# By rows out of a layer: two projections of a transformer kernel give tokens in rows, and the norms behind them are postponed

## The chip, the cores and the metric

One NeuronCore of a Trainium2 chip runs the whole program. The metric is the device time of one execution in microseconds; the median of several runs is given. The engines are TensorE (PE: matmul, with PEld for its weight loads), VectorE (DVE), ScalarE (ACT), GpSimd (POOL) and SyncE (SP), which issues the DMAs.

## What is computed

A transformer of three layers on 256 tokens of width 1024, all in fp32. The first layer (block 1) has three kinds of attention and a gated feed-forward with a causal convolution; the next two (block 2) are modulated by a condition vector `c`. Only the ends of the first layer and the start of the second matter here:

```python
def rmsnorm(x, g):
    y = xf * lax.rsqrt(jnp.mean(xf * xf, axis=-1, keepdims=True) + EPS) * g

# first_block
mixed = concatenate([rmsnorm(out_a, g_a), rmsnorm(out_b, g_b), rmsnorm(out_c, g_c)])
x = x + rmsnorm(mixed @ w_out, attn_post_norm)
h = rmsnorm(x, ffn_pre_norm)
u = causal_depthwise_conv(h @ w_up, conv_w, conv_b)      # 3 taps, 5632 columns
gate, up = split(u, 2)
x = x + rmsnorm((gelu(gate) * up) @ w_down, ffn_post_norm)  # 2816 -> 1024

# second_block, for layer in 0, 1
shift_m, scale_m, gate_m, shift_f, scale_f, gate_f = split(silu(c) @ ada_w + ada_b, 6)
h = rms_norm(x, norm_gains[layer, 0]) * (1 + scale_m) + shift_m
x = x + gate_m * mixer(h)          # layer 0: w_qkv, attention, w_o
h = rms_norm(x, norm_gains[layer, 1]) * (1 + scale_f) + shift_f
x = x + gate_f * swiglu(h)         # gate_up, down
```

## The kernel before

**Layout.** Activations stand turned: a tile is 128 features on the partitions by S = 256 tokens, and x is DT = 8 such tiles. A matrix product takes a 128 x 128 block of weights as the stationary operand and streams 256 tokens. For accuracy each fp32 operand is split in two reduced-precision parts, `hi` (a rounded copy, made by ACT) and `lo` (the remainder, made by DVE), and each product is three matmuls: hi x hi, lo x hi, hi x lo (L1334 to L1336). PE's time is the count of these matmuls.

**Chunks.** Weights come in chunks. `PHASES` lists the layers in order with their chunks: w_in 10, w_out 5, up 22, down 16, qkv 12, att_o 4, gu0 22, dn0 16, ret_in 24 and so on. For each chunk SP issues a load into a ring of raw buffers (L582), ACT makes `w_hi` from it (L729), DVE `w_lo` (L2014), each in two halves of up to 1024 columns, and PE then works the chunk: for a chunk of 1 MB 48 matmuls of 256 columns. `hi(chunk)` and `lo(chunk)` are the two splits; each engine's order is written out by hand, and they stand one chunk ahead. A load waits till the raw buffer's last chunk is split.

**PSUM.** The eight banks are `lin[0:2]`, `sco[0:2]`, `tra[0:2]` and `att[0:2]`. A layer's chunks use `lin` in turn. A chunk's bank is free once its reader has left it: in up that are DVE's convolution taps (L2249).

**Up.** For each pair of feature tiles ACT starts the convolution (L964 on) from the bank, DVE adds two taps for each tile, ACT makes gelu, GpSimd (two chunks of three) or DVE multiplies by the up half (L652), and ACT rounds the hidden tile (L993), GpSimd takes its remainder (L662). The modulation of block 2 is worked in 48 pieces of 1 MB, spread over the layers (`ADA_STEPS`): SP loads a piece (L572) after the chunk's weights, waiting till DVE has finished the piece two before, and DVE makes two products with sums (L2098) and a small addition behind the chunk's split and taps.

**Norms.** A norm needs the sum of squares of each token, over the partitions. ACT squares each tile, PE multiplies it by ones into one column (`sums`, L1431), DVE refines 1/sqrt from ACT's root and writes two 128 x 128 diagonals of the factors (L2023 to L2030), and PE multiplies ones by these (`spread`, L1443), which gives the factors on all partitions. In between PE runs fillers on constant data (`keep_busy`, L1412). The residual norms POST (behind w_out) and FFNPOST (behind down) then scale y by the factors and add it to x, tile by tile (L2078). Behind each follows another norm of the new x: FFNPRE before up, L0 before qkv, again with squares, sums, factors, spread, and for each of eight tiles scale, round, remainder. Up's and qkv's chunk 0 goes by feature tiles in the order in which these are ready.

**Postponed norms.** Three norms further on (`DEFERRED`: L0F before gu0, L1, L1F) are treated another way. The next layer's chunks 0 to 2 run on z = x * gain, not normalised, with banks of their own (L1709 `start_chunk`). Chunk 0 has the sums at one of its 16 places, chunk 1 has the spread at its place 0 (L1731 `deferred_phase`). ACT copies the factors (`rbc_copy`) and the three chunks' banks into SBUF (`leave_first`, L1112), and GpSimd multiplies these six tiles by the factors (`settle`, L682). Meanwhile DVE scales eight tiles of h (L2324, L2329), with chunk 2's split after tiles 4 and 6 and chunk 3's behind them (L2313), and from chunk 3 on the layer runs on h. GpSimd adds the squares of the tiles first (L642), so that fewer sums stand on PE.

**Order around w_out.** The last group of mixed tiles (late norm GROUP_F) comes during w_out's first two chunks; its spread stands behind two chunks of 36 matmuls. The loads of up wait for its last tile, since up's buffers lie where these were made.

## Time and profile before

| | us |
|---|---|
| median of 3 runs | 1107.26 |
| lowest and highest of them | 1104.3, 1260.35 |
| the profiled execution as a run | 1108.74 |
| its span (first to last instruction) | 1106.9 |
| mean granted TensorE clock in it | 0.989 |

The profile is one execution. Its page gives busy time of each engine, a picture of the span in 40 slices, DMA queues, the chain of work that ended last, groups of instructions and DMA issues. Durations below come from it. The trace also answers for single instructions (a timeline) and for stretches (windows). A busy PE may be doing fillers, and a matmul's shown duration overlaps the next one's: the pace is the distance between starts. In the windows "PEclk" is the granted clock, 1.00 for 2.4 GHz and 0.50 for 1.2 GHz, and the DMA share is the mean over the core's 16 DMA engines.

### The profile page before, as it was taken

The numbers are of one execution on the slowest core, as the hardware profiler recorded it, in microseconds if no ns is written. First come the engines' busy times: TensorE is split into PE (matmuls) and PEld (weight loads), VectorE is DVE, ScalarE is ACT, GpSimd is POOL, SyncE is SP. The second block draws the span as 40 slices with busy tenths as digits, with TensorE's granted clock in tenths as the row PEclk, the third lists the DMA queues.
The fourth block names the chain that finished last, engine by engine and source line by source line (L and its number), as shares of the span: only waits on it lengthen the run. The fifth ranks groups of instructions, "written<-read, shape, count | busy, mean of one in ns | idle before, by whom it ended". The sixth has DMA issues, their size and how long they took to land.

```text
span 1106.9 us, 21659 instructions
## 1 busy us (share of the span) xinstructions
PE 1065.8 (96%) x8385; PEld 1027.9 (93%) x8385; DVE 792.3 (72%) x1375; ACT 596.0 (54%) x1016; POOL 142.3 (13%) x146
## 2 busy tenths in 40 slices
PE   6989999999989999999999999999999999999998
PEld 5878899999989999799999999997899999999997
DVE  5767658999978788768887788877467657554443
ACT  6576446776444456657544444633465556544442
POOL 0000012434310000003211101300010013111010
PEclk9999989999999899999999999999999999999999
DMA  9621263767498553345797778454334454554450
GB/s 365 222 86 68 77 259 154 295 239 287 166 363 321 227 215 128 115 176 179 304 353 281 282 291 332 173 215 162 143 138 148 179 183 153 190 189 154 159 182 38
DMA packets 34399, 226.66 MB, mean 205 GB/s; under 512 B 3827, under 2 KB 4124, under 8 KB 12444
## 3 DMA queue, kind: packets, MB, share of 16 engines
q1 hardware_dynamic: 33884, 223.11, 53.8%
q0 software_dynamic: 448, 2.63, 0.6%
q8 instruction: 45, 0.74, 0.3%
q14 instruction: 22, 0.18, 0.0%
HBM read 224.66 MB, written 2.63 MB: 205 GB/s over the span
## 4 chain that ended last, share of the span: by engine, by line
PE 77%; DVE 9%; ACT 5%; DMA 5%; issue 2%; POOL 1%; SPq 0%; DVEq 0%; ACTq 0%; POOLq 0%
PE psum L1334 21%; PE psum L1336 20%; PE psum L1335 20%; DVE w_lo L2014 3%; DMA raw<-in_down 2%; PE psum L1399 2%; PE psum L1402 2%; PE psum L1401 2%; PE psum L1412 2%; DVE arena L2098 2%; ACT w_hi L729 2%; PE psum L1431 1%; POOL arena L682 1%; DMA raw<-in_qkv 1%; DMA raw<-in_up 1%
## 5 line engine op out<-in xcount | busy, mean ns | idle before, releaser
L2014 DVE TENSOR_TENSOR w_lo<-raw,w_hi 128x1024 fp32r<-128x1024 f32 (+1 forms) x354 | 395.9, 1141 | 202.4 <-ACT w_hi L729 195.5
L729 ACT ACTIVATE w_hi<-raw 128x1024 fp32r<-128x1024 f32 (+1 forms) x354 | 338.3, 971 | 264.6 <-PE psum L1336 201.7
L1334 PE MATMUL psum<-h_hi,w_hi 128*128 128x256 f32 (+1 forms) x1240 | 355.3, 287 | 6.8 <-DVE w_lo L2014 3.0
L1335 PE MATMUL psum<-h_lo,w_hi 128*128 128x256 f32 (+1 forms) x1240 | 349.2, 282 | 0.0
L1336 PE MATMUL psum<-h_hi,w_lo 128*128 128x256 f32 (+1 forms) x1240 | 347.9, 281 | 0.0
L1334 PE MATMUL psum<-hid_hi,w_hi 128*128 128x256 f32 (+1 forms) x1096 | 311.8, 284 | 14.2 <-DVE w_lo L2014 7.7
L1336 PE MATMUL psum<-hid_hi,w_lo 128*128 128x256 f32 (+1 forms) x1096 | 309.9, 283 | 0.0
L1335 PE MATMUL psum<-hid_lo,w_hi 128*128 128x256 f32 (+1 forms) x1096 | 309.6, 283 | 0.0
L1334 PEld LDWEIGHTS psum<-h_hi,w_hi 128*128 128x128 f32 x1240 | 233.4, 188 | 11.2 <-issue 5.8
L1335 PEld LDWEIGHTS psum<-h_lo,w_hi 128*128 128x128 f32 x1240 | 234.5, 189 | 0.7 <-issue 0.7
L1336 PEld LDWEIGHTS psum<-h_hi,w_lo 128*128 128x128 f32 x1240 | 234.5, 189 | 0.0
L1334 PEld LDWEIGHTS psum<-hid_hi,w_hi 128*128 128x128 f32 x1096 | 207.3, 189 | 16.9 <-issue 11.1
L1336 PEld LDWEIGHTS psum<-hid_hi,w_lo 128*128 128x128 f32 x1096 | 207.1, 189 | 0.0
L1335 PEld LDWEIGHTS psum<-hid_lo,w_hi 128*128 128x128 f32 x1096 | 207.0, 189 | 0.0
L2098 DVE CUSTOM_DVE_ANT_0 arena<-arena 128x1024 f32<-128x1024 f32 x96 | 124.3, 1331 | 0.0
L642 POOL TENSOR_TENSOR arena<-arena 128x256 f32<-128x256 f32 x29 | 29.4, 1013 | 475.4 <-ACT arena L1102 322.2
L993 ACT ACTIVATE hid_hi<-arena 128x256 f32 (+1 forms) x60 | 25.1, 418 | 79.2 <-DVE arena L2259 63.4
L662 POOL TENSOR_TENSOR hid_lo<-arena,hid_hi 128x256 f32 (+1 forms) x44 | 35.9, 816 | 181.6 <-ACT hid_hi L993 173.4
L1412 PE MATMUL psum<-busy 128*128 128x256 f32 x221 | 40.3, 343 | 2.5 <-ACT busy L768 2.5
L652 POOL TENSOR_TENSOR arena<-arena 128x256 f32<-128x256 f32 x22 | 31.2, 1419 | 86.5 <-ACT arena L982 86.5
L1412 PEld LDWEIGHTS psum<-busy 128*128 128x128 f32 x221 | 36.4, 246 | 3.0 <-ACT busy L768 2.5
L2249 DVE SCALAR_TENSOR_TENSOR arena<-psum,cols,arena 128x255 f32<-128x255 f32 (+1 forms) x88 | 36.3, 473 | 1.7 <-ACT arena L972 1.1
(245 smaller groups left out, 1024.9 us busy)
## 6 DMA issues: line engine op xcount, KB each, us to landing
arena<-in_ada SPq DMA_DIRECT2D x48, 1024.0 KB, 4.9
raw<-in_gu SPq DMA_DIRECT2D x44, 1024.0 KB, 4.8
raw<-in_ret_in SPq DMA_DIRECT2D x24, 1024.0 KB, 4.8
raw<-in_up SPq DMA_DIRECT2D x22, 1024.0 KB, 7.0
raw<-in_dn SPq DMA_DIRECT2D x32, 704.0 KB, 5.5
raw<-in_qkv SPq DMA_DIRECT2D x12, 1024.0 KB, 7.8
raw<-in_down SPq DMA_DIRECT2D x16, 704.0 KB, 7.1
raw<-in_ret_o SPq DMA_DIRECT2D x8, 1024.0 KB, 4.7
```

The source lines that it names most:

```text
L642: nc.gpsimd.tensor_tensor(acc, acc, sq[:, k * S:(k + 1) * S], ALU.add).then_inc(sq_added, 1)
L652: nc.gpsimd.tensor_tensor(hid, ff["u"][:, 2 * at + S:2 * at + 2 * S], ff["g"][:, at:at + S], ALU.mult)\
L662: nc.gpsimd.tensor_tensor(hid_lo[:, cut], ff["hid"][:, S * (j % 2):S * (j % 2) + S], hid_hi[:, cut].bitcast(F32), ALU.subtract).then_inc(h ...
L729: nc.scalar.activation(w_hi[chunk % SPLIT_SLOTS][:, a:b], raw[chunk % RAW_SLOTS][:, a:b], ACT.Copy)\
L993: nc.scalar.activation(hid_hi[:, bass.ds(step.n(lambda c: (c - lag) * S), S)], ff["hid"][:, S * (j % 2):S * (j % 2) + S], ACT.Copy).then_i ...
L1334: nc.tensor.matmul(out, w[0], hc, start=start, stop=False, skip_group_check=True)
L1335: nc.tensor.matmul(out, w[0], lc, start=False, stop=False, skip_group_check=True)
L1336: return nc.tensor.matmul(out, w[1], hc, start=False, stop=stop, skip_group_check=True)
L1412: nc.tensor.matmul(bank[:, 0:S], busy[:, 0:P], busy[:, :], start=True, stop=True)
L2014: tt(w_lo[s][:, a:b], raw[chunk % RAW_SLOTS][:, a:b], w_hi[s][:, a:b].bitcast(F32), ALU.subtract)\
L2098: ins = nc.vector.tensor_tensor_reduce(w, w, cond_silu, 1.0, 0.0, ALU.mult, ALU.add, sums[:, b:b + 1])
L2249: ins = stt(u[:, back:S], bank[:, S * s:S * s + S - back], w, u[:, back:S], ALU.mult, ALU.add)
```

## The change

1. **Rows.** w_out (4 chunks now) and down (11 chunks of 1 MB, before 16 of 704 KB) use the activation tiles as the stationary operand (128 features x 128 tokens) and stream 512 columns of weights: `by_rows`. The result has tokens on the partitions and stands in four banks: rows 0 in `sco`, rows 1 in `lin`. In the last chunk the banks are finished one after the other.
2. **The residual norms** POST and FFNPOST are gone as norms. ACT squares each bank with an accumulation along the row (`row_squares`), DVE makes the factors (`row_residual`) and a diagonal for each 128 tokens; copies of the rows (`row_copies`) are multiplied by the diagonals on PE, 16 fp32 matmuls of 128 columns (`turn_rows`), which turns them back into feature tiles and normalises them. x gets turned * gain, tile by tile.
3. **The norms behind them**, FFNPRE and L0, join `DEFERRED`. As DVE updates each tile of x, ACT makes z's hi part and the square, and DVE the lo part. For these two the sums stand at place 1 and the spread at place 11 of chunk 1. In up the first three chunks' convolution reads the settled tiles (`conv_settled`, `taps_settled`), in qkv `settle_heads` makes q and k of them, and the first attention scores move from chunks 3 and 4 to chunk 4.
4. **Pieces.** Up has a piece at chunks 5, 6, 7, 9, 11 ... 19, 20, 21 (before: each odd one), down one at each of chunks 0 to 9 (before 11 over 16 chunks), qkv none (before 3), gu0 one at each of chunks 4 to 20 (before 13).

```diff
-    ("w_in", 10, DT, 2, 1), ("w_out", 5, DT, 2, 1),
-    ("up", 22, DT, 2, 1), ("down", 16, HALF, 1, 2),
+    ("w_in", 10, DT, 2, 1), ("w_out", 4, DT, 2, 1),
+    ("up", 22, DT, 2, 1), ("down", 11, DT, 2, 1),
...
-ADA_STEPS = [("w_in", 10, lambda c: int(c in (KA, QA0))), ("up", 22, lambda c: c % 2), ("down", 16, lambda c: int(c % 2 or c in (0, 2, 12))),
-             ("qkv", 12, lambda c: int(c < 3)),
-             ("gu0", 22, lambda c: int(4 <= c <= 20 and (c % 2 or c in (4, 6, 8, 18, 20)))), ("dn0", 16, lambda c: c % 2)]
+ADA_STEPS = [("w_in", 10, lambda c: int(c in (KA, QA0))), ("up", 22, lambda c: int(c >= 5 and c % 2 or c in (6, 20))),
+             ("down", 11, lambda c: int(c < 10)), ("gu0", 22, lambda c: int(4 <= c <= 20)), ("dn0", 16, lambda c: c % 2)]
...
-NORM_GROUPS = [[8], [2, 1], [4, 2], [2], [8], [8], [8], [8], [8], [8], [8], [8]]
+NORM_GROUPS = [[8], [2, 1], [4, 2], [2], [], [8], [], [8], [8], [8], [8], [8]]
...
-DEFERRED = (L0F, L1, L1F)
+DEFERRED = (FFNPRE, L0, L0F, L1, L1F)
...
+            def row_squares(ph, i):
+
+                stage = ROW_STAGE[i]
+                for r in range(2):
+                    for n in range(2):
...
+                        at = 28 + 2 * n + r
+                        nc.scalar.activation(e0["sq"][:, (2 * r + n) * 512:(2 * r + n + 1) * 512], row_bank(ph, r, n)[:, :], ACT.Square,
+                                             scale=D ** -0.5, accum_out=row_stat[:, at:at + 1]).then_inc(row_sq, 1)
+                act.wait_ge(row_ms, stage + 1)
+                nc.scalar.activation(row_stat[:, 6:8], row_stat[:, 0:2], ACT.Sqrt).then_inc(row_root, 1)
+                leave(nc.scalar.activation(row_of(1, 1), row_bank(ph, 1, 1)[:, :], ACT.Copy), ph.unit0 + 1)
...
             hi(PH["up"].chunk0)
-            for p in range(4):
-                post_unit(p)
+            row_squares(PH["w_out"], FFNPRE)
             hi(SPLIT_AHEAD[FFNPRE], ahead=0)
-            warm_root(POST)
-            root(POST)
+            rows_by_gains(FFNPRE)
             hi(SPLIT_AHEAD[FFNPRE], ahead=1)
...
+            conv_settled(0)
+            leave_first(ph, FFNPRE, 2, (0,))
+            conv_settled(1)
+            leave_first(ph, FFNPRE, 2, (1,))
+            hi(ph.chunk0 + 4)
+            gelu(Step(2))
+            round_hid(Step(2), 2)
+            conv_settled(2)
+            gelu(Step(3))
+            round_hid(Step(3), 2)
...
+            def by_rows(ph, c, ready=None):
+
+                whi, wlo = weights(ph.chunk0 + c, Step(c), ph)
+                last = c == ph.n - 1
+                if last:
+                    order = [(k, r, n) for r in range(2) for n in range(2) for k in range(2)]
+                else:
+                    order = [(k, r, n) for k in range(2) for r in range(2) for n in range(2)]
...
+                    nc.tensor.matmul(bank[:, :], hid_hi[:, t:t + P], whi[:, w], start=c == 0 and k == 0, stop=False, skip_group_check=True)
+                    nc.tensor.matmul(bank[:, :], hid_lo[:, t:t + P], whi[:, w], start=False, stop=False, skip_group_check=True)
+                    ins = nc.tensor.matmul(bank[:, :], hid_hi[:, t:t + P], wlo[:, w], start=False, stop=last and k == 1, skip_group_check=True)
...
+            def turn_rows(ph, i):
+
+                stage = ROW_STAGE[i]
+                keep_busy(18, att[1])
+                units_done(pe, ph.unit0 + 2)
+                pe.wait_ge(row_copied, 2 * (stage + 1))
+                for k in range(DT):
+                    for r in range(2):
...
+                        ins = nc.tensor.matmul(turned_rows(k)[:, r * P:(r + 1) * P], e0["y"][:, r * D + k * P:r * D + (k + 1) * P],
+                                               row_diag_of(r), start=True, stop=True)
...
+            swiglu_phase("up", FFNPRE, 1, 11)
+            ph = PH["down"]
+            for c in range(ph.n):
+                pe.wait_ge(hid_tiles, 2 * c + 2)
+                by_rows(ph, c)
+            turn_rows(ph, L0)
+
+            deferred_phase("qkv", L0, 1, spread_at=11)
...
+            def row_residual(ph, i, gain_):
...
+                for k in range(DT):
+                    if k % 2 == 0:
+                        dve.wait_ge(row_turned, DT // 2 * stage + k // 2 + 1)
+                    cut = slice(k * S, (k + 1) * S)
+                    stt(x[:, cut], turned_rows(k), gain_(k), x[:, cut], ALU.mult, ALU.add).then_inc(row_x, 1)
+                    if k:
+                        rest_of(k - 1)
+                rest_of(DT - 1)
...
+            taps_settled(0)
+            taps_settled(1)
+            lo(ph.chunk0 + 4)
+            taps_settled(2)
+            steps(dve, ph.n, 8, 1, up_step)
```

## Rows read from the trace of the kernel before

**Rows 1.** The page, section 1: busy us, share of the span, instructions.

```profile
PE 1065.8 (96%) x8385; PEld 1027.9 (93%) x8385; DVE 792.3 (72%) x1375; ACT 596.0 (54%) x1016; POOL 142.3 (13%) x146
```

**Rows 2.** Windows by stage: us; PE, PEld, DVE, ACT, POOL busy; PEclk, DMA, GB/s.

```profile
118.90:143.20 24.30, 24.30 (x204) 24.30 (x205) 14.77 (x29) 11.89 (x21) 1.15 (x1) 1.00 0.47 172
143.20:170.30 27.10, 25.11 (x173) 24.76 (x173) 15.92 (x40) 11.63 (x29) 2.52 (x4) 0.81 0.47 190
170.30:292.50 122.20, 121.89 (x1014) 120.66 (x1013) 114.90 (x179) 86.76 (x133) 46.51 (x41) 1.00 0.60 235
292.50:363.70 71.20, 64.47 (x530) 63.20 (x530) 56.47 (x89) 31.37 (x52) 7.72 (x7) 1.00 0.84 329
363.70:389.20 25.50, 24.19 (x171) 23.49 (x171) 20.16 (x48) 11.01 (x24) 0.00 (x0) 0.87 0.44 181
535.00:570.00 35.00, 35.00 (x294) 35.00 (x293) 33.24 (x49) 16.77 (x26) 6.67 (x7) 1.00 0.87 336
```

**Rows 3.** PE timeline: start us, us, engine, line, operation, count; first junction.

```profile
156.26 3.66 PE L1431 MATMUL psum<-ones,arena 128*128 128x1 f32 x32
```

**Rows 4.** SP and ACT timeline: first load of up.

```profile
131.26 2.08 SPq L582 DMA_DIRECT2D raw<-in_up  x2
...
139.48 2.01 ACT L729 ACTIVATE w_hi<-raw 128x1024 fp32r<-128x1024 f32 x2 [4.01 <-DMA raw<-in_up]
```

**Rows 5.** PE timeline: ten issues 512 columns wide, first and last.

```profile
791.48 0.40 PE L1401 MATMUL psum<-w_lo,hid_hi 128*128 128x512 f32 x1
...
793.81 0.39 PE L1402 MATMUL psum<-w_hi,hid_lo 128*128 128x512 f32 x1
```

**Rows 6.** DVE timeline: a norm's factors, and a split in halves.

```profile
149.17 0.16 DVE L2023 TENSOR_SCALAR stat<-psum 128x2 f32<-128x2 f32 x1 [0.63 <-PE psum L1431]
...
150.38 0.48 DVE L2030 TENSOR_SCALAR diag<-ident,stat 128x128 f32<-128x128 f32 x2
...
171.50 2.36 DVE L2014 TENSOR_TENSOR w_lo<-raw,w_hi 128x1024 fp32r<-128x1024 f32 x2 [2.00 <-ACT w_hi L729]
```

**Rows 7.** DVE timeline: remainders for the norm before gu0.

```profile
498.90 2.65 DVE L2310 SCALAR_TENSOR_TENSOR hid_lo<-x,gscale,hid_hi 128x256 fp32r<-128x256 f32 x4
...
503.35 0.89 DVE L2310 SCALAR_TENSOR_TENSOR hid_lo<-x,gscale,hid_hi 128x256 fp32r<-128x256 f32 x2 [0.90 <-ACT hid_hi L1100]
```

**Rows 8.** PE and DVE timeline: postponed norm before gu0.

```profile
508.45 0.61 PE L1443 MATMUL psum<-diag,ones 128*128 128x128 f32 x4
...
509.51 0.88 DVE L2324 SCALAR_TENSOR_TENSOR arena<-x,gscale,arena 128x256 f32<-128x256 f32 x2 [1.40 <-ACT arena L1122]
...
515.94 0.36 PE L1334 MATMUL psum<-hid_hi,w_hi 128*128 128x258 f32 x1 [1.12 <-DVE w_lo L2014]
```

**Rows 9.** Groups by line (the page, section 5, and by form): busy, mean ns.

```profile
L2098 DVE CUSTOM_DVE_ANT_0 arena<-arena 128x1024 f32<-128x1024 f32 x96 | 124.3, 1331 | 0.0
...
L652 POOL TENSOR_TENSOR arena<-arena 128x256 f32<-128x256 f32 x22 | 31.2, 1419 | 86.5 <-ACT arena L982 86.5
...
L2249 DVE SCALAR_TENSOR_TENSOR arena<-psum,cols,arena 128x255 f32<-128x255 f32 (+1 forms) x88 | 36.3, 473 | 1.7 <-ACT arena L972 1.1
...
L682 POOL TENSOR_TENSOR arena<-arena 128x256 f32<-128x256 f32 x18 | 20.6, 1174 | 49.3 <-ACT arena L1112 49.3
```

**Rows 10.** SP and ACT timeline in down; page, section 6: KB, us to landing.

```profile
300.77 0.43 SPq L582 DMA_DIRECT2D raw<-in_down  x1
...
306.94 1.47 ACT L729 ACTIVATE w_hi<-raw 128x768 fp32r<-128x768 f32 x2 [5.29 <-DMA raw<-in_down]
...
arena<-in_ada SPq DMA_DIRECT2D x48, 1024.0 KB, 4.9
...
raw<-in_down SPq DMA_DIRECT2D x16, 704.0 KB, 7.1
```

**Rows 11.** PE timeline and window: an idle stretch, and what follows.

```profile
60.48 0.36 PE L1334 MATMUL psum<-hid_hi,w_hi 128*128 128x256 f32 x1 [3.26 <-ACT arena L839]
...
61.90:65.20 3.30, 3.30 (x18) 2.70 (x18) 1.23 (x1) 2.77 (x5) 0.00 (x0) 0.50 0.00 0
```

More of the change, by code:

```diff
@@ L211, with nth @@
 SPLITS = [PRE, LATENT, GROUP, GROUP_F, FFNPRE, L0, L0F, L1, L1F]
-RESIDUALS = [POST, FFNPOST, FINAL]
+def nth(norm):
+    return sum(bool(NORM_GROUPS[i]) for i in range(norm + 1))
 def norm_tiles(norm):
@@ L252, in additions @@
 def additions(norm, n):
[L254 removed]
+    if norm in (PRE, GROUP):
         return 0
```

523 lines of the change are left out of this document (265 added, 258 removed).

## The prediction

> **What bounds the kernel now.** I read the page first. TensorE (PE) is busy for 96% of the span [rows 1], so no other engine is the bound over the whole; what a change can win or lose are the stretches where PE runs no work of the reference. The table by stage says where those lie [rows 2]. Between the first block's layers there are two junctions: 27.1 us from the last matmul of w_out (143.2) to the end of up's chunk 0 (170.3), and 25.5 us from the last matmul of down (363.7) to the end of qkv's chunk 0 (389.2). A chunk is 48 matmuls of 256 columns, some 5.8 us, so the junctions hold about 21 and 20 us of norms, in which PE does sums (32 records of one column in 3.66 us [rows 3]), spreads and fillers. The granted clock of those stretches is 0.81 and 0.87, a mix of the 1.2 and 2.4 GHz levels. Up itself is dense: 21 chunks in 122.2 us, 5.82 each, but DVE is busy there for 114.9 us, 94%. Down takes 71.2 us for 528 matmuls, which at 0.119 us would be 62.8: the table has the DMA queues at 0.84, and ACT's splitting waits on weights. So a norm can be postponed to PE's profit only if DVE, ACT, GpSimd and the DMAs keep up behind it.
>
> **The change, part by part.**
>
> *Wider matmuls.* Both layers now stream weights, 512 columns at a time. Ten issue intervals of that shape take 2.33 us, 0.233 each [rows 5], against 2 x 0.119 for two of 256. w_out: 96 x 0.233 = 22.4 instead of 192 x 0.119 = 22.8, so its last matmul comes at about 142.7. Down would be 264 x 0.233 = 61.5 if nothing held it. The sum over both is a gain below 2 us.
>
> *Junction w_out to up.* ACT splits up's chunk 0 before it squares the rows. SP starts that load only after the last h tile of the late norm; the spread before that tile will stand after two chunks by rows, 118.9 + 48 x 0.233 + 0.9 for the sums = 131.0; now it stands after two chunks of 36 narrow matmuls, 118.9 + 72 x 0.119 + 0.9 = 128.4, so the load of 131.26 goes out at 133.8 and lands 8.2 us later as now [rows 4], at 142.0. ACT is then held till 144.1 by the two halves (2.01 us), after the last matmul. Queued behind it are four squares of 512 columns with accumulation; a half of 1024 columns takes 1.0 there, so I put them at 0.7 each with the accumulator's read (bounds 0.5 and 1.0): till 146.9. From there the factors take what they take now, 149.17 to the first diagonal's end at 150.62, 1.45 us [rows 6]: 148.4. PE turns rows back: 16 fp32 matmuls, two records each, about 0.1 us a record by the spread's four in 0.61 [rows 8], so 0.85 us for the first two tiles; then x update, ACT's rounding, DVE's remainder: first z tile 151.0. Each further tile costs DVE an update and a remainder. The trace has such remainders at 0.44 us where GpSimd rests and at 0.66 where it adds squares [rows 7]; updates are like 0.44. GpSimd will add squares all through, so the bounds are 0.85 and 1.1 a tile; I take 1.0. The Trainium skill (GPSIMD Engine Reference, Key points) says that GpSimd shares its SBUF interfaces with VectorE and contends with instructions of two SBUF inputs; by that the pace would be 1.1 throughout and the junction 0.7 us longer; the first of the two rows agrees. The last z tile is ready at 158 to 159 (PE may turn at the lower clock after its idle time from 144.9 to 148.4), DVE then splits half of chunk 1, 1.2 us, and chunk 1 starts at S = 160.0. Now it starts at 170.3: **-10.3**. Bounds: 158 if the load lands early, 161.5 with 1.1 a tile and a slow turn.
>
> *What the postponed norm costs in up.* The nearest rows are the existing postponed norm before gu0 [rows 8]: the spread at 508.45, DVE's first scaled tile at 509.51 (call it V), chunk 2 on PE at 515.94 = V + 6.4, after a wait of 1.1 us for w_lo, because DVE splits chunk 2 only between scaled tiles. There the spread opens chunk 1. Here the sums stand at place 1 of 16 and the spread at place 11, so V = S + 0.36 + 0.8 + 3.6 + 0.4 + 0.6 = S + 5.8. Chunk 1, with sums and spread, is over at S + 7.0; chunk 2 starts at V + 6.4 = S + 12.2. PE idles 5.3 us there. Then the settled chunks. GpSimd multiplies six tiles at 1.17 each from V + 8.8, first pair at 11.1; ACT copies conv chunk 0 (two of about 0.5) to 12.2, leaves half a bank, PE's chunk 3 starts at V + 12.7. ACT: conv 1 to 14.4, leave 14.8, split of chunk 4 16.8, table load 18.1, gelu 18.5; GpSimd product 1.42 [rows 9] 19.9; ACT rounding 20.4, conv 2 21.4, gelu 21.8; product 23.2; rounding 23.7; split of chunk 5 25.7, gelu 26.1, conv 3 27.1; DVE's taps, 4 x 0.47 less overlap, 28.8. Chunk 5 needs chunk 3's bank, which those taps free: it starts at V + 28.9 = S + 34.7 = 194.7, where PE could have started it at V + 24.3. Now chunk 5 starts at 170.3 + 4 x 5.82 = 193.6: so at this point all 10.3 us are given back and **1.1** more. The bounds of this term are the existing norm's loss (chunk 3 some 2.7 us late, then nothing: 11 us better) and 3 us worse with a second table load and slower products.
>
> *The rest of up.* 17 chunks at 5.76 are 97.9, now 98.9. Pieces of the modulation (two products of 1.33 mean on DVE [rows 9]) now come in threes, at 5, 6, 7 and 19, 20, 21: a step of split 2.3, taps 1.6 and piece 2.5 is 6.4 against 5.76, about 0.7 us late each, 1.4 in all beyond the present slips. An idle stretch of 3.3 us before 60.48 is followed by a stretch at granted clock 0.50, the 1.2 GHz level [rows 11]; two idle stretches of about 5 us will do the same, the first hidden by the ACT chain, the second costs half of 3.4 us, 1.7. Up ends at 194.7 + 97.9 + 1.4 + 1.7 = 295.7 instead of 292.5: **+3.2** so far.
>
> *Down.* SP's order is load(c), piece(c), load(c+1); piece(c) waits until DVE has finished piece(c-2). So load(c+1) cannot go out before piece(c-2) is done, and it feeds the split of c+1, after which DVE works piece(c). Now 11 pieces lie over 16 short chunks; after, every chunk 0 to 9 has one, so two chunks share one such loop: issue 0.6, landing T, two-part split 3.45 (ACT's first half 1.1, then DVE's 2.36 [rows 6]), piece 2.5. For T: a load of 0.72 MB issued right behind a piece took 6.14 us (300.77 to ACT's start at 306.94), the median of in_down is 7.1 [rows 10]; 1.05 MB behind 1.05 MB I put at 7.0, bounds 6.2 and 9. The Trainium skill (DMA: Bandwidth & Descriptors, Anatomy of one DMA) gives a fixed 2.0 us plus bytes at 436 GB/s, by which the pair of 2.1 MB takes an estimated 6.8; by that the sum is 1 us less. Loop = 13.55 us for two chunks, 6.8 a chunk, against 5.6 on PE. From up's last piece, 4.5 us after down's start: chunk 2 at 4.5 + 0.6 + 7.0 + 2.3 = 14.4, chunk 10 at 14.4 + 4 x 13.55 = 68.6, its end at 74.2, and 0.8 because qkv's loads share the last one: 75.0 instead of 71.2. **+3.8.**
>
> *Junction down to qkv.* Here ACT is free and the table is warm: last matmul, square 1.2, factors to 2.75, first z tile 5.35, last 12.35, half split, chunk 1 starts at 13.7 (S') instead of 25.5: -11.8. Then the same late spread: chunk 2 at V + 6.4; chunk 3 at V + 12.2 = 18.0 after S' where 11.5 is its due: +6.5; lower clock after the idle stretch +1.5. The chain of ACT and GpSimd is not in PE's way here, since only DVE's settling of q and k waits. **-3.8.**
>
> *Later.* Three pieces leave qkv (PE had no waits there, nothing gained) and four go to gu0, where six in a row already run at DVE 33.2 of 35 us with PE full [rows 2]: hidden; with no cover each would cost its 2.5 us.
>
> Sum: 3.2 + 3.8 - 3.8 = **+3.2 us** on the span of 1106.9, 1110.1. That execution took 1108.7 as a run, 1.8 around the span; the median shown is 1107.3, so I forecast **1110.5 us**.
>
> **Rivals.**
> *The postponed norms hide as the three existing ones do* (chance 0.15). For: those sites lose only 2 us of waits each [rows 8]. Against: their spread stands first, and they have no convolution. Then up's first part gains 10.3 + 1.1 - 2.5 = about 9, qkv 11.8 - 3.2 = 8.6, and down, with T near 6.2, costs 0: 1107 - 18 = 1089.
> *Down isn't held by the loop* (0.2): loads land in 5.5 us behind a piece because the DMA queues carry less at once. Chunk 10 then starts at 4.5 + 0.6 + 5.5 + 2.3 + 4 x 12.05 = 61.1 and down takes 66.7, 4.5 us less than now; with all else as forecast 1102. For: in_ada's 1 MB has a median of 4.9 [rows 10]. Against: 6.14 with less data.
> *The loop alone makes it slower* (0.12): the loads of down, each behind a piece, land in 9 us. Chunk 2 at 4.5 + 0.6 + 9 + 2.3 = 16.4, chunk 10 at 16.4 + 4 x (9 + 6.55) = 78.6, its end at 84.2, and 0.8 for qkv's loads: 85.0, +13.8; beside the forecast's +3.8 that is 10 more, 1121 in total. It decides from T = 8 on; over 2% only beyond T = 10.5. For: the median of in_down is 7.1 now, with 704 KB [rows 10]. Against: behind a piece, the place that counts, it was 6.14.
> *The change doesn't postpone anything in effect*, PE being held all the same: that is my forecast's own reading of up.
>
> **Chances.** Forecast 0.53, range of its own 1103 to 1118. With the rivals: faster by over 2% (below 1085, about what a measurement of this kernel tells from no change) 0.10, from the lower part of the first rival and from its falling together with the second (1089 - 4.5 = 1084.5); slower by over 2% (above 1129) 0.05, from the upper part of the third; within 0.85. Below 1089 I see about 1 in 10, and above 1123 too: the range is 1089 to 1123.
>
> **What would show it.** Right: PE waiting some 5 us for w_lo before chunk 2 of up and of qkv, and 3 to 5 us before chunk 5 of up for DVE's taps; up's chunk 1 starting near 160; ACT's w_hi waiting on DMA in down, chunks 6.8 us apart; clock 0.5 behind the idle stretches. Wrong: chunk 1 before 157 or no wait before chunk 5 (up's term off by up to 11); down's chunks at 5.6 us (off by 10); GpSimd or DVE making PE wait in gu0.

## The result, and the profile after

The changed kernel takes 1113.3 us (median of 8 runs, 1111.9 to 1119.5) against 1108.0 for the kernel before on the same chips: ratio 1.0066, 95% interval 1.0040 to 1.0093, so 5 to 7 us slower (the medians differ by 5, the ratio gives 7) and within 2%. The ratio leaves out one execution of the kernel before that took 1260.35 us. The forecast was 1110.5 us with a range of 1089 to 1123. The profiled execution of the changed kernel took 1112.1 us as a run, its span is 1110.3 us. The page's first section, which answers [rows 1], shows that PE is busy for less of the span, 94% after 96%. A part of that is no loss: fillers fell from 221 matmuls to 121, and two norms' sums are gone. The rest shows in the stages:

```profile
PE 1047.6 (94%) x7901; PEld 991.6 (89%) x7901; DVE 809.1 (73%) x1392; ACT 588.4 (53%) x1014; POOL 156.6 (14%) x162
```

The table by stage, with the changed kernel's own boundaries, answers [rows 2] line by line (w_out; its junction; up from chunk 1; down; its junction to qkv's chunk 1; the same stretch of gu0). Columns as there: us, busy time of PE, PEld, DVE, ACT, POOL, granted clock, DMA share, GB/s.

```profile
117.10:141.00 23.90, 23.90 (x110) 19.68 (x111) 12.66 (x27) 9.58 (x17) 0.00 (x0) 1.00 0.36 140
141.00:155.20 14.20, 11.94 (x98) 11.37 (x96) 12.39 (x29) 10.66 (x27) 4.50 (x6) 1.00 0.47 196
155.20:294.80 139.60, 126.36 (x1020) 124.92 (x1020) 124.33 (x196) 82.06 (x139) 48.00 (x45) 0.96 0.57 224
294.80:370.60 75.80, 66.45 (x267) 51.18 (x266) 59.65 (x89) 29.20 (x40) 7.26 (x6) 0.95 0.83 318
370.60:384.00 13.40, 12.44 (x100) 11.65 (x98) 11.59 (x28) 9.60 (x22) 4.50 (x6) 1.00 0.29 105
538.40:573.40 35.00, 35.00 (x294) 35.00 (x293) 34.76 (x51) 16.77 (x26) 6.93 (x7) 1.00 0.86 334
```

The junctions have shrunk from 27.1 and 25.5 us to 14.2 and 13.4. Up from chunk 1 has grown from 122.2 to 139.6 us, and PE has no work in 13 of them; down has grown from 71.2 to 75.8. gu0's stretch is as full as before, with DVE at 34.8 of 35 us.

The start of w_out varies by some 4 us from execution to execution in all profiles here (116.3 to 120.4 us), before any edit can act. So stages are compared from w_out's first matmul, counted on PE's timeline, up to the first matmul of gu0's chunk 2, which waits 1.1 us for w_lo in every profile as in [rows 8]. Behind that point both kernels take 591.0 us (515.94 to 1106.9, and 519.31 to 1110.3). Times in us from w_out's first matmul, then the length of down, and from down's last matmul to that point of gu0:

| profile | up chunk 1 | chunk 3 | chunk 5 | chunk 9 | up's end | down | to gu0 | sum |
|---|---|---|---|---|---|---|---|---|
| before | 51.6 | 63.2 | 75.0 | 98.2 | 173.4 | 71.1 | 152.5 | 397.1 |
| changed | 38.2 | 58.1 | 72.2 | 100.7 | 177.8 | 75.5 | 149.0 | 402.3 |

The sum is 5.2 us longer, as the medians say. In the experiments' profiles the part behind that point takes 590.9 to 594.3 us, though no edit lies there (595.4 in experiment 10, which has one more piece in gu0), so up to 3.4 us between two times can come from it; the table leaves it out. The gain of 13.4 us at up's chunk 1 has become 2.8 at chunk 5, a loss of 2.5 at chunk 9 and of 4.4 at up's end. PE's timeline shows where it waits (the bracket is the idle time before the instruction and what ended it):

```profile
145.24 3.81 PE L1729 MATMUL psum<-diag,arena 128*128 128x128 f32 x32 [2.14 <-DVE diag L2133]
...
167.18 0.55 PE L1345 MATMUL psum<-hid_hi,w_hi 128*128 128x256 f32 x1 [4.65 <-DVE w_lo L2052]
...
189.25 0.58 PE L1345 MATMUL psum<-h_hi,w_hi 128*128 128x256 f32 x1 [2.63 <-DVE arena L2346]
...
210.15 0.39 PE L1345 MATMUL psum<-h_hi,w_hi 128*128 128x256 f32 x1 [2.19 <-DVE arena L2346]
...
217.76 0.38 PE L1345 MATMUL psum<-h_hi,w_hi 128*128 128x256 f32 x1 [1.69 <-DVE arena L2346]
...
302.64 0.80 PE L1711 MATMUL psum<-w_hi,hid_hi 128*128 128x512 f32 x1 [4.24 <-DVE arena L2346]
...
344.69 0.47 PE L1711 MATMUL psum<-w_hi,hid_hi 128*128 128x512 f32 x1 [0.81 <-DVE w_lo L2052]
...
373.67 3.81 PE L1729 MATMUL psum<-diag,arena 128*128 128x128 f32 x32 [0.77 <-DVE diag L2133]
...
396.46 0.55 PE L1345 MATMUL psum<-hid_hi,w_hi 128*128 128x258 f32 x1 [5.08 <-DVE w_lo L2052]
```

### The profile page after: what moved, and what is told of

It is laid out like the page before. It is cut to its first block, busy times and chain, and to the rows that moved or that the text cites. A ratio compares the mean times of both kernels' runs of the same rounds, so it can differ in the third digit from the quotient of the medians.

```text
span 1110.3 us, 20499 instructions
## 1 busy us (share of the span) xinstructions
PE 1047.6 (94%) x7901; PEld 991.6 (89%) x7901; DVE 809.1 (73%) x1392; ACT 588.4 (53%) x1014; POOL 156.6 (14%) x162
## 4 chain that ended last, share of the span: by engine, by line
PE 69%; DVE 14%; ACT 6%; DMA 6%; issue 2%; POOL 2%; SPq 0%; DVEq 0%; ACTq 0%; POOLq 0%
PE psum L1345 18%; PE psum L1347 18%; PE psum L1346 18%; DVE w_lo L2052 5%; DMA raw<-in_down 4%; ACT w_hi L746 3%; DVE arena L2156 2%; PE psum L1410 2%; PE psum L1413 2%; PE psum L1412 2%; POOL arena L699 1%; DMA raw<-in_up 1%; DVE arena L2307 1%; DVE arena L2346 1%; DVE hid_lo L2137 1%
## 5 line engine op out<-in xcount | busy, mean ns | idle before, releaser
L746 ACT ACTIVATE w_hi<-raw 128x1024 fp32r<-128x1024 f32 (+1 forms) x342 | 334.3, 997 | 258.6 <-PE psum L1347 173.4
L1345 PE MATMUL psum<-h_hi,w_hi 128*128 128x256 f32 (+1 forms) x1144 | 328.0, 287 | 14.6 <-DVE arena L2346 8.6
L1346 PE MATMUL psum<-h_lo,w_hi 128*128 128x256 f32 (+1 forms) x1144 | 322.8, 282 | 0.0
L1347 PE MATMUL psum<-h_hi,w_lo 128*128 128x256 f32 (+1 forms) x1144 | 321.6, 281 | 0.0
L1345 PE MATMUL psum<-hid_hi,w_hi 128*128 128x256 f32 (+1 forms) x952 | 273.2, 287 | 15.9 <-DVE w_lo L2052 12.5
L1347 PE MATMUL psum<-hid_hi,w_lo 128*128 128x256 f32 (+1 forms) x952 | 270.4, 284 | 0.0
L1346 PE MATMUL psum<-hid_lo,w_hi 128*128 128x256 f32 (+1 forms) x952 | 270.4, 284 | 0.0
L1347 PEld LDWEIGHTS psum<-hid_hi,w_lo 128*128 128x128 f32 x952 | 181.4, 191 | 0.0
L659 POOL TENSOR_TENSOR arena<-arena 128x256 f32<-128x256 f32 x33 | 29.3, 887 | 455.0 <-ACT arena L1143 261.1
L1711 PE MATMUL psum<-w_hi,hid_hi 128*128 128x512 f32 x120 | 49.7, 414 | 10.9 <-DVE arena L2346 5.2
L1712 PE MATMUL psum<-w_hi,hid_lo 128*128 128x512 f32 x120 | 48.4, 403 | 0.0
L1713 PE MATMUL psum<-w_lo,hid_hi 128*128 128x512 f32 x120 | 48.3, 403 | 0.0
```

The costliest lines, as they stand in the source:

```text
L659: nc.gpsimd.tensor_tensor(acc, acc, sq[:, k * S:(k + 1) * S], ALU.add).then_inc(sq_added, 1)
L746: nc.scalar.activation(w_hi[chunk % SPLIT_SLOTS][:, a:b], raw[chunk % RAW_SLOTS][:, a:b], ACT.Copy)\
L1345: nc.tensor.matmul(out, w[0], hc, start=start, stop=False, skip_group_check=True)
L1346: nc.tensor.matmul(out, w[0], lc, start=False, stop=False, skip_group_check=True)
L1347: return nc.tensor.matmul(out, w[1], hc, start=False, stop=stop, skip_group_check=True)
L1711: nc.tensor.matmul(bank[:, :], hid_hi[:, t:t + P], whi[:, w], start=c == 0 and k == 0, stop=False, skip_group_check=True)
```

## The experiments

Each is the changed kernel with the edit named, if not said otherwise. Ratios are to the kernel before, run on the same chip. The rows of all experiments in the units of the table above:

| profile | up chunk 1 | chunk 3 | chunk 5 | chunk 9 | up's end | down | to gu0 | sum | ratio, 95% |
|---|---|---|---|---|---|---|---|---|---|
| changed | 38.2 | 58.1 | 72.2 | 100.7 | 177.8 | 75.5 | 149.0 | 402.3 | 1.0066 (1.0040-1.0093) |
| 1 late pieces in down | 39.4 | 59.0 | 73.4 | 100.7 | 177.0 | 68.6 | 149.2 | 394.8 | 0.9984 (0.9959-1.0009) |
| 2 spread at 5 | 39.3 | 55.2 | 71.5 | 99.9 | 176.9 | 75.9 | 146.7 | 399.4 | 1.0022 (0.9999-1.0046) |
| 3 up not postponed | 48.1 | 59.6 | 71.2 | 98.1 | 175.5 | 75.8 | 148.1 | 399.4 | 1.0037 (1.0009-1.0064) |
| 4 late pieces in up too | 39.9 | 59.7 | 73.9 | 99.7 | 176.7 | 69.2 | 148.0 | 393.9 | 0.9976 (0.9955-0.9997) |
| 5 last piece behind taps | 38.4 | 58.3 | 72.4 | 100.8 | 177.7 | 82.6 | 148.7 | 409.0 | 1.0108 (1.0087-1.0129) |
| 6 edits 2, 4, 5 together | 38.3 | 55.7 | 70.5 | 96.6 | 173.9 | 65.5 | 146.2 | 385.6 | 0.9913 (0.9889-0.9937) |
| 7 as 6, up not postponed | 48.3 | 59.8 | 71.2 | 97.1 | 174.7 | 66.6 | 144.9 | 386.2 | 0.9886 (0.9865-0.9908) |
| 8 as 7, qkv neither | 49.9 | 61.5 | 73.0 | 98.9 | 175.7 | 66.3 | 149.7 | 391.7 | 0.9932 (0.9909-0.9955) |
| 9 as 7, pieces apart | 50.3 | 61.8 | 73.4 | 96.4 | 172.9 | 63.0 | 145.0 | 380.8 | 0.9860 (0.9829-0.9892) |
| 10 as 6, nine pieces | 38.4 | 55.8 | 70.6 | 93.7 | 170.9 | 62.8 | 149.7 | 383.3 | 0.9933 (0.9909-0.9957) |
| 11 before, late pieces | 50.9 | 62.3 | 74.2 | 97.5 | 172.9 | 66.0 | 151.4 | 390.2 | 0.9923 (0.9898-0.9948) |
| 12 as 9, more fillers | 48.1 | 59.7 | 71.0 | 94.1 | 170.0 | 62.8 | 145.8 | 378.6 | 0.9849 (0.9810-0.9887) |

One column needs a caution: the turn behind w_out runs at the full clock in some executions and partly at half in others, after the same idle stretch, which moves everything behind it by 1 to 2 us (experiment 12).

### 1. The loop of the pieces in down

```diff
-                    late = 2 if ph.name == "gu0" else 0
+                    late = 2 if ph.name in ("gu0", "down") else 0
...
-                for c in (20, 21) if ph.name == "gu0" else ():
+                for c in (ph.n - 2, ph.n - 1) if ph.name in ("gu0", "down") else ():
```

> The changed kernel, with one edit: in down SP issues the modulation piece of chunk c behind the weight load of chunk c+2 instead of behind that of chunk c. Theory (the loop piece(c-2) -> load(c+1) -> split -> piece(c) paces down at 6.6 us a chunk): without the loop down's 11 chunks go at 5.6, down takes 66 to 67 us instead of 75.7, and the span falls by 9, from 1110 to about 1101. Rival (the DMA queues are full, 2.1 MB a chunk): the chunks stay above 6.3 us, and the span falls by 3 at most.

The loop itself can be read from the changed kernel's timeline (SP issues, ACT's and DVE's splits, the small addition that ends a piece):

```profile
301.05 0.33 SPq L596 DMA_DIRECT2D arena<-in_ada  x1
...
301.43 0.42 SPq L606 DMA_DIRECT2D raw<-in_down  x1
...
334.86 0.16 DVE L2159 TENSOR_TENSOR mod<-ada_sums,cols 128x2 f32<-128x2 f32 x1
...
335.05 0.33 SPq L596 DMA_DIRECT2D arena<-in_ada  x1
...
335.42 0.43 SPq L606 DMA_DIRECT2D raw<-in_down  x1
...
342.22 2.00 ACT L746 ACTIVATE w_hi<-raw 128x1024 fp32r<-128x1024 f32 x2 [4.64 <-DMA raw<-in_down]
...
343.32 2.36 DVE L2052 TENSOR_TENSOR w_lo<-raw,w_hi 128x1024 fp32r<-128x1024 f32 x2 [1.81 <-ACT w_hi L746]
...
348.00 0.16 DVE L2159 TENSOR_TENSOR mod<-ada_sums,cols 128x2 f32<-128x2 f32 x1
...
348.19 0.33 SPq L596 DMA_DIRECT2D arena<-in_ada  x1
...
348.56 0.43 SPq L606 DMA_DIRECT2D raw<-in_down  x1
```

The addition of one piece ends at 335.0, SP issues the next piece at 335.05 and only then the load at 335.42; ACT gets it at 342.22, 6.8 us later; DVE's split ends at 345.7, the piece behind it at 348.2, and SP issues again at 348.19. That is 13.1 us for two chunks, 6.6 each, where PE needs 5.6. With late pieces down took 68.6 us instead of 75.5, its chunks 1 to 10 ran 5.57 us apart, and PE was busy through all of them:

```profile
307.00:362.00 55.00, 55.00 (x239) 44.59 (x238) 47.95 (x71) 23.21 (x27) 0.00 (x0) 1.00 0.90 346
```

The theory held, and the rival (chunks above 6.3 us) fell. The edit was worth 7 us in the trace, not 9: 5.2 us of waits at down's start stayed (experiment 5), and behind them the first chunk lost another 2.3 us at the lower clock. The queues carried 346 GB/s in this stretch, at a share of 0.90; experiment 6 shows that they carry more.

### 2. The place of the spread

```diff
-            swiglu_phase("up", FFNPRE, 1, 11)
+            swiglu_phase("up", FFNPRE, 1, 5)
...
-            deferred_phase("qkv", L0, 1, spread_at=11)
+            deferred_phase("qkv", L0, 1, spread_at=5)
```

> The changed kernel, with one edit: the spread of the postponed norm stands at place 5 of chunk 1 instead of 11, in up and in qkv. Theory (the chain spread -> scaled tiles -> split of chunk 2 -> settling -> convolution gives the time back): spread and everything behind it come 2 us earlier at both places, the wait of chunk 2 falls from 4.7 and 5.1 us to 2.7 and 3.1, up ends 2 us earlier, and the span is 4 us shorter, 1106. Rival (up is bound by DVE's total work, so an earlier spread in it is given back): only qkv gains, and the span is 2 us shorter or less.

```profile
159.73 0.88 DVE L2307 SCALAR_TENSOR_TENSOR arena<-x,cols,arena 128x256 f32<-128x256 f32 x2 [1.03 <-ACT arena L968]
...
165.69 0.35 PE L1345 MATMUL psum<-hid_hi,w_hi 128*128 128x256 f32 x1 [2.48 <-DVE w_lo L2052]
...
187.78 0.38 PE L1345 MATMUL psum<-h_hi,w_hi 128*128 128x256 f32 x1 [3.59 <-DVE arena L2346]
```

The first scaled tile (L2307) came 4.2 us behind chunk 1's start (155.55) instead of 6.0, and the wait before chunk 2 fell from 4.65 to 2.48 us. Chunk 5 started at 187.78, that is 28.05 us behind the first scaled tile; in the changed kernel it was 189.25 - 161.22 = 28.03, and in experiments 5 and 6 it is 28.04 and 28.06. So the chain to chunk 5 is fixed behind the spread, as the theory says. Against w_out's first matmul that tile was only 0.7 us earlier, since this execution's turn behind w_out ran slow and moved chunk 1 by 1.1 us; chunk 5 was 0.7 us earlier too, and up's end 0.9. The 2.9 us at chunk 3 contain another gain that the chain took back: behind the shorter wait chunk 2 ran at full clock (5.8 us instead of 8.0). In qkv 2.3 us stayed. Up's end was to come 2 us earlier by the theory and came 0.9 earlier, 2.0 if the 1.1 us of the slow turn are added back. So the trace bears the theory out with that correction; the ratio fell from 1.0066 to 1.0022, and the intervals overlap.

### 3. Rows without postponing, before up

The norm before up leaves `DEFERRED`; ACT squares each updated tile of x, and PE does sums, spread and fillers before chunk 0, as in the kernel before. Its core:

```diff
-DEFERRED = (FFNPRE, L0, L0F, L1, L1F)
+DEFERRED = (L0, L0F, L1, L1F)
...
-            swiglu_phase("up", FFNPRE, 1, 11)
+            norm(FFNPRE, 16, bank=lin[1])
+            by_feature(PH["up"], Step(0), (h_tiles, tiles_before(FFNPRE)))
```

> The changed kernel, but the norm before up is not postponed: w_out still gives rows that are turned back by diagonals, then squares, sums, factors, spread and eight scaled tiles come before up's chunk 0, as in the kernel before. qkv is as in the changed kernel. Theory (postponing gives all its gain back in up, the rows alone save one half of the junction): chunk 1 of up starts at about 163 instead of 155.2, chunk 5 at about 187 instead of 189.3, up runs at 5.8 us a chunk and ends at 287 to 290 instead of 294.8; the span falls by 5 to 8, to 1103. Rival (postponing does pay in up): up ends after 295, and the span is 1111 or more.

Chunk 1 came at 48.1 us, 3.5 before the kernel before and 9.9 behind the changed one; at chunk 5 it was 1.0 ahead of the changed kernel, and up ended 2.3 us earlier. So all that postponing gained at chunk 1 was gone at chunk 5. Yet up's end was 2.1 us later than in the kernel before, although chunk 5 was 3.8 earlier: 5.9 us were lost behind chunk 5 without any postponed norm. That loss was the surprise, and its largest waits are before chunks 8 and 9 (1.8 and 1.6 us), where the pieces stand three in a row. By my expectation up would have ended 5 to 8 us earlier than in the changed kernel, by the rival later than there; it was 2.3 us earlier, so neither held in size. The ratio, 1.0037 against 1.0066, doesn't separate the two kernels.

### 4. Late pieces in up too

```diff
-                    late = 2 if ph.name in ("gu0", "down") else 0
+                    late = 2 if ph.name in ("gu0", "down", "up") else 0
...
-                steps(sp, ph.n, *{"up": (8, 0), "gu0": (12, 1)}.get(ph.name, (4, 0)), one)
+                steps(sp, ph.n, *{"up": (10, 0), "gu0": (12, 1)}.get(ph.name, (4, 0)), one)
```

> The changed kernel with the pieces issued two chunks late in down and in up. Against the run with down alone it tells what the same loop costs in up, where chunk 8's load goes out late behind the pieces of chunks 5, 6, 7: theory, the waits before chunks 8 and 9 of up (2.2 and 1.7 us) go, and the span is 3 to 4 us under that of the run with down alone. Rival (DVE is the bound there): the waits move on by a chunk or two, and the gain is below 1 us.

In the changed kernel ACT waited 5.0 us for chunk 8's weights (split at 205.08), because SP had issued that load behind the piece of chunk 7. Here that wait went, but the one before chunk 9 stayed at 1.27 us. From chunk 5 to chunk 9 it took 25.8 us instead of 28.5 (and 27.3 in experiment 1); at up's end 0.3 us were left against experiment 1, and the ratios (0.9976 and 0.9984) do not differ. The comparison with one edit between them is that with experiment 1: 1.5 us up to chunk 9. Experiment 1 has the changed kernel's up unedited and still took 1.2 us less there, where chunk 8's load landed in 6.7 us instead of 7.9. The rival held for the larger part: DVE is behind, not only the loads.

### 5. The last piece of up behind the last taps

```diff
                 taps(step)
-                if c < ph.n:
+                if c < ph.n and (step.i is not None or c < ph.n - 1):
                     pieces(ph.name, step)
...
             lo(PH["down"].chunk0 + 1)
+            pieces(ph.name, Step(ph.n - 1))
```

> The changed kernel, with one edit: on DVE the piece of up's chunk 21 stands behind the last taps and the split of down's chunk 1, where it stood before the last taps. By rows, down's chunk 0 needs both banks of lin, and its second one waited 4.2 us for those taps. Theory (the loop of the pieces paces down, so that this wait is hidden behind it): the 4.2 us wait goes, but the load of down's next chunk now goes out later, and down's chunk 10 starts as late as before, within 1 us of 69.7 us after down's start: the time stays within 2 us of the changed kernel's 1113.3. Rival (the wait adds to the end): 4 us less, 1109.

```profile
301.85 0.50 PE L1711 MATMUL psum<-w_hi,hid_hi 128*128 128x512 f32 x1 [2.08 <-DVE arena L2346]
...
307.47 0.16 DVE L2159 TENSOR_TENSOR mod<-ada_sums,cols 128x2 f32<-128x2 f32 x1
...
307.66 0.33 SPq L596 DMA_DIRECT2D arena<-in_ada  x1
...
308.04 0.42 SPq L606 DMA_DIRECT2D raw<-in_down  x1
...
371.88 0.77 PE L1711 MATMUL psum<-w_hi,hid_hi 128*128 128x512 f32 x1 [3.02 <-DVE w_lo L2052]
```

The wait for the second bank of lin fell from 4.24 to 2.08 us, as it should. But the piece of chunk 21 ended 11.4 us behind down's start (307.6) instead of 6.2, so SP issued the next piece and the load behind it at 307.66 and 308.04 instead of 301.05 and 301.43. Chunk 10 started 75.7 us behind down's start instead of 69.7, and the kernel became slower than the changed one: 409.0 us to gu0 instead of 402.3, a ratio of 1.0108 instead of 1.0066. Both forecasts for this run were wrong; I had counted the wait and not the 5.2 us by which the loop's first piece would come later. It is strong evidence for the loop: 5.2 us later on DVE were 6 us later at chunk 10, although PE had been given 2 us.

### 6 to 8. Which norm is worth postponing

Experiment 6 joins edits 2, 4 and 5; experiment 7 adds edit 3 to it; experiment 8 takes the norm before qkv out of `DEFERRED` as well, with qkv's first chunks, copies and first scores as in the kernel before.

> The changed kernel with three edits together: pieces issued two chunks late in up and down, the spread at place 5 of chunk 1 in up and qkv, and the piece of up's chunk 21 behind the last taps. Both norms stay postponed. Theory: the run with late pieces in up and down took 393.9 us from w_out's first matmul to chunk 2 of gu0; without the loop the wait at down's start now adds to the end, so its 4.2 us come off, 2.2 come off by the spread in qkv and 1 in up: 386.5, and 1098 to 1100 as a run. Rival (each edit's gain is given back at the next bound, DVE in up, the DMA queues in down): 391 or more, 1103 and up.

> As the run with three edits, but the norm before up is not postponed (rows and diagonals stay). Theory (postponing gives all back in up: chunk 5 stands 28.0 us behind the first scaled tile, whatever the spread's place): chunk 5 starts 71.2 us after w_out's first matmul, up ends at 173 to 174 instead of 176, and the run takes 1096 to 1098, 2 us under the run with three edits. Rival (the postponed form is at least as good once the pieces are out of the way): the same time or 1 to 3 us more than with three edits.

> As the run before this one, but the norm before qkv isn't postponed either; both layers still give rows that the diagonals turn back, so this is the rows' part of the change alone, with late pieces. Theory: rows save 3 us of a junction against the form before; from the end of down to chunk 3 of qkv it takes 34 us, against 36.1 in the changed kernel and 33.9 with the spread at 5, so the time is that of the run with qkv alone postponed, 1096 to 1098. Rival (postponing pays in qkv, where ACT and GpSimd have room): 2 us or more slower than the run with qkv alone postponed.

Once the pieces were issued late, the edit of experiment 5 did what it was meant to: down took 65.5 us against 69.2 in experiment 4, and the sum, 385.6, came within 1 us of the forecast for it. The chip could carry what down asks: for 44 us the DMA queues were nearly full, and PE still did not wait.

```profile
309.70:354.00 44.30, 44.29 (x191) 35.94 (x192) 41.91 (x64) 18.20 (x19) 0.00 (x0) 1.00 0.99 410
```

Experiment 7 kept its chunk 5 at 71.2 us to the digit, but up's end, 174.7, was no better than 173.9 with the norm postponed: by the trace its rival held, postponing in up neither gains nor loses. The medians (1101.4 and 1096.7) lean to the theory and differ more than the sums do, but the intervals overlap, and in the profiled executions 4.1 us of the difference lie before w_out and 3.3 behind gu0's chunk 2, where the two kernels are alike.

Experiment 8 against 7 gives the worth of postponing before qkv: 149.7 instead of 144.9 us from down's end to gu0, 4.8 us, and the times agree (0.9932 against 0.9886, intervals that just part). Its own theory, that both would be alike, fell. It had put 34 us from down's end to qkv's chunk 3 and the run took 34.7; what was wrong was the 33.9 for the postponed form with the spread at 5. That is the figure of the changed kernel (404.2 - 370.35); with the spread at 5 it was 31.6 in experiment 2 and 29.3 in experiment 7. The rows alone save 1.7 us there against the kernel before with late pieces (151.4, experiment 11) and 2.8 against the kernel before as it stands (152.5); behind w_out they save up to 3.5 (51.6 to 48.1).

### 9 and 10. Where the pieces stand

```diff
-             ("up", 22, lambda c: int(c >= 5 and c % 2 or c in (6, 20))),
+             ("up", 22, lambda c: c % 2),
```

> As the run in which only the norm before qkv is postponed (late pieces, spread at 5, last piece behind the taps), but up's 11 pieces stand at the odd chunks, as in the kernel before. Theory (three pieces in a row at chunks 5 to 7 and 19 to 21 make DVE late, which costs the waits before chunks 8 and 9, 1.3 us each, and smaller ones later): up ends at 171 to 172 us after w_out's first matmul instead of 174.7, and the run takes 3 us less than 1096.7. Rival (the sum of DVE's work in up counts, not where the pieces stand): the waits appear at other chunks, and the gain is below 1 us.

> As the run with three edits (both norms postponed), but up has 9 pieces, at the odd chunks from 5 on; the two others go to down's last chunk and to gu0's. Theory: with room on DVE for chunks 5 to 8 the waits before chunks 8 and 9 (1.4 and 1.3 us) shrink to under 1 us in sum, up ends at 171 to 172 after w_out's first matmul instead of 173.7, down and gu0 are as before, and the run takes 2 us less than with three edits. Rival (the chain to chunk 5 has made DVE and ACT late and the waits stay): no gain.

With up's eleven pieces at the odd chunks, the stretch from chunk 5 to up's end took 99.5 us instead of 103.5; in the kernel before it is 98.4. PE had one wait of 0.8 us left in it. In experiment 10 (pieces at 5, 7 ... 21, one more at down's last chunk and one at gu0's) it took 100.3 instead of 103.4. So pieces in a row cost 4 us of up where the norm is not postponed (experiment 9 has as many pieces as 7, only their places differ). With the postponed norm 3 us came back, but experiment 10 also has two pieces fewer in up, and place and amount are not told apart there. Experiment 10 lost its gain again at once, by a term that I had put at nothing:

```profile
354.15 1.22 DVE L2156 CUSTOM_DVE_ANT_0 arena<-arena 128x1024 f32<-128x1024 f32 x1
...
356.63 1.88 DVE L2120 COPY arena<-psum 128x512 f32<-128x512 f32 x3
...
360.07 5.36 PE L1729 MATMUL psum<-diag,arena 128*128 128x128 f32 x32 [3.52 <-DVE diag L2133]
```

The piece at down's last chunk (354.15) stands before the copies of the rows (356.63) on DVE. PE's turn waited 3.5 us for the diagonal instead of 0.3 in experiment 6, and then took 5.36 us instead of 3.8: from down's end to gu0 it took 149.7 us instead of 146.2.

### 11. The late pieces without the change

The kernel before with edit 1 in down.

> The kernel before, with one edit: in down the pieces are issued two chunks late. It tells how much of the best run's gain belongs to the late pieces alone. Theory: down's waits for w_lo (2.5, 1.5 and 0.9 us) go, down takes 66 to 67 us instead of 71.4, and the run takes 1103 to 1104. Rival (those waits are for the DMA queues, whose share is 0.84 there): 1107 to 1108, as before.

Down took 66.0 instead of 71.1 us, and the time fell by 0.8%. The theory held: of the three waits one of 0.6 us was left. So the kernel before had the same loop, at 11 pieces in 16 chunks. Late pieces alone make 0.8% of the 1.5% that the best kernel here gains (experiment 12), and the rest is the change's with its pieces and norm rearranged.

This run also tells whether the loop is what makes the change slower. With late pieces in down on both sides (experiments 1 and 11) the sums are 394.8 and 390.2 us, 4.6 apart, where with the loop on both sides they are 402.3 and 397.1, 5.2 apart. Of the 4.6 us, 4.1 stand at up's end already, 2.6 come in down, and 2.2 are won back behind it. So the loop costs both kernels about the same, and most of the change's own loss lies in up.

### 12. The idle stretch before the turn

```diff
-                keep_busy(18, att[1])
+                keep_busy(34 if i == FFNPRE else 22, att[1])
```

> As the run with pieces apart, with one edit: before the rows are turned back PE runs 34 fillers instead of 18 behind w_out, and 22 behind down, so that its idle stretch of 2.1 to 2.4 us before the turn behind w_out is filled. In the profiles taken so far the turn behind w_out took 3.8 us six times and 5.3 to 5.4 us five times, with the same idle stretch before it. Theory (the idle stretch decides the clock of the turn): the turn takes 3.8 us, chunk 1 of up starts 48.3 us after w_out's first matmul instead of 50.3, and the time is 1 to 2 us under 1094.7, less than the timing resolves. Rival (the granted clock there is not set by that idle stretch): 5.4 us again in the profile, and the same time.

The turn's 32 records in experiment 9, and here:

```profile
148.28 5.44 PE L1719 MATMUL psum<-diag,arena 128*128 128x128 f32 x32 [2.31 <-DVE diag L2125]
```

```profile
142.45 4.22 PE L1413 MATMUL psum<-busy 128*128 128x256 f32 x34
...
146.99 3.81 PE L1719 MATMUL psum<-diag,arena 128*128 128x128 f32 x32 [0.31 <-DVE diag L2125]
```

It took 3.81 us, and chunk 1 came at 48.1 us instead of 50.3. One profile can't show that the idle stretch decides it, since 6 of the 11 profiles before also had 3.8 us; the time, 0.9849 against 0.9860, does not resolve it. It is the fastest kernel of the study: 1092.3 us against 1109.0, 1.5% under the kernel before and 2.2% under the changed one by the ratios.

## Why the prediction was right, and where it was not

The time fell in the range and the sign was right. That the number came so near is in part luck: the first junction was 3.1 us better than forecast and the stretch behind chunk 5 was 5.1 us worse, and in down two errors cancelled. By terms, in us, measured from w_out's first matmul:

| step | forecast | measured |
|---|---|---|
| junction w_out to up's chunk 1 | -10.3 | -13.4 |
| chunk 1 to chunk 5, postponed norm | +11.4 | +10.6 |
| chunk 5 to up's end | +2.1 | +7.2 |
| down | +3.8 | +4.4 |
| down's end to gu0 | -3.8 | -3.5 |
| sum | +3.2 | +5.2 |

**Junction, mis-sized by 3.** The order of events was as told, but the load of up's chunk 0 took 6.4 us and not the 8.2 of [rows 4]:

```profile
132.01 2.84 SPq L606 DMA_DIRECT2D raw<-in_up  x4
...
138.43 2.01 ACT L746 ACTIVATE w_hi<-raw 128x1024 fp32r<-128x1024 f32 x2 [5.37 <-DMA raw<-in_up]
```

Its split was over at 140.4, before w_out's last matmul (140.55), so the squares followed the matmuls at once, 0.71 us each (forecast 0.7), and were over at 142.74. The factors then waited on DVE, which copied three banks of rows first (141.80 to 143.68), 0.9 us that the forecast did not have; the first diagonal stood at 145.05. That is 1.5 us of it. The tiles then came 0.87 us apart, not 1.0: DVE's updates took 0.48 and its remainders 0.48 to 0.58 (the last 0.79), although GpSimd added squares meanwhile. The 0.66 us of [rows 7] were not reached. The Trainium skill (GPSIMD Engine Reference, Key points) has GpSimd contend with VectorE's two-input instructions; here the remainder rose from 0.48 to 0.56 us once GpSimd added squares, a smaller effect than [rows 7] had made me expect.

**The postponed norm in up, right.** The first scaled tile, V, came 6.0 us behind chunk 1's start (forecast 5.8), chunk 2 at V + 6.0 (6.4) after a wait of 4.65 (5.3), and chunk 5 at V + 28.0 (28.9), after a wait that ended with DVE's taps. That wait was 2.6 us, less than the 3 to 5 forecast, because chunk 2 took 8.0 us at a granted clock of 0.69. Experiment 2 moved V and chunk 5 moved with it. Which of ACT, GpSimd and DVE makes the chain that long was worked out in the forecast; no run changed one of them alone. The reading of the trace of the existing postponed norm in [rows 8] carried this far; what it could not show was the convolution's chain, and the durations in [rows 9] did.

**Behind chunk 5, the step that failed.** I gave pieces in threes 1.4 us and the lower clock 1.7. The clock was right: chunk 5 took 7.3 us instead of 5.8, 1.5 more, at a granted clock of 0.77.

```profile
189.20:196.50 7.30, 7.25 (x49) 7.25 (x49) 6.82 (x13) 4.06 (x7) 2.81 (x3) 0.77 0.00 0
```

The pieces' term was too small by 4 to 5 us. I had counted DVE's work per step (6.4 us against 5.76), but not that the loop which I described for down also stands in up, where three pieces follow one another: chunk 8's load left SP behind the piece of chunk 7. Experiment 4 gives the loads' share (1.5 us at chunk 9 against experiment 1, 2.7 against the changed kernel), of which DVE takes most back: 0.3 us were left at up's end. Experiment 9 gives the pieces' places with the loads already early, 4.0 us. Two smaller waits, 0.8 us at chunk 13 and 1.0 at chunk 17, come and go: experiment 10 has both, experiment 9 one, experiment 12 none above 0.3 us. Their cause is open.

**Down, right in size, partly by luck.** The loop ran at 6.6 us a chunk (forecast 6.8), with 6.8 us from issue to ACT where I took 7.0, but only from chunk 5 on, so chunks 2 to 10 took 50.0 us where the forecast had 54.2. Against that, chunk 2 started 19.7 us behind down's start and not 14.4: the first chunk took 14.1 us instead of 5.6. 5.2 us of this were waits, and 3.3 us the lower clock behind them (a granted clock of 0.53 from 302.6 to 308.9 us); I had seen neither. Rows need both banks of lin in down's first chunk, and the second one is free only after the taps of up's last chunk, which stand behind a piece. That delay let the loads run ahead, and chunks 1 to 4 ran at 5.6 to 5.9 us. Two errors of 5.3 and 4.2 us with opposite signs left the sum right; experiment 5 shows that the two costs don't add up freely, and experiment 6 that both can be taken away. The estimate from the Trainium skill (DMA: Bandwidth & Descriptors, Anatomy of one DMA), whose figures are fitted to transfers issued by GpSimd, was 6.8 us for the pair of transfers; these are issued by SP, and the trace has 7.2 us from the first issue of a pair (335.05) to ACT's start (342.22), 6.8 from the second, so it agrees within 0.4.

**The junction to qkv, right.** Chunk 1 stood 13.4 us behind down's last matmul (forecast 13.7), chunk 2 waited 5.1 us (5.3), and behind it the granted clock was 0.52 between 395.9 and 401.0 us. The time was not given back by ACT or GpSimd, as told, because PE doesn't wait for the settled tiles there.

**The rivals.** That the norms hide as the existing ones do is wrong for up. For qkv it is wrong in size: 3.5 us were gained up to gu0, 5.8 with the spread at place 5, where the rival had 8.6. Its sum of 1089 also counts 1.1 us too much: by its own losses up's first part gains 10.3 - 2.5, not 10.3 + 1.1 - 2.5. That down isn't held by the loop was wrong as the kernel stands. That the loop alone makes it slower has a mechanism that is there, but not its size (loads landed in 6.8 us, not 9) nor its conclusion. Without the loop the changed kernel is level with the kernel before (0.9984), but that kernel gains as much when its own loop goes (0.9923), and 4.6 of the 5.2 us between them stay (experiment 11). My forecast for down, +3.8 us, put the change's loss in the same wrong place: 2.6 of the 4.4 us in down stay without the loop, and up's 4.4 us, of which I had 3.2, are the larger part. That GpSimd or DVE would make PE wait in gu0 did not happen.

## What to carry to other kernels

Postpone a norm where the engines that must make up for it have room and where PE doesn't wait for their result: the same transformation was worth 4.8 us before qkv and nothing before up. There DVE had 6% of the time free, and PE's banks waited for a convolution on the settled tiles; the runs don't tell which of the two counts more. Read the order of a queue that issues two kinds of transfer as a loop: if one kind waits for an engine that itself works behind the other kind, its period is the sum of the whole way round, and taking a wait away on the busiest engine gains nothing until that loop is cut, and costs if the edit puts the loop's work later. Before a loss is put down to such a loop, cut the loop in the kernel before as well: here both had it. When work is redistributed with a change, cost its place as well as its amount, above all next to a junction, where a piece of 2.5 us cost 3.5.
